# One operand of the first branch product: split ahead of its phase, or loaded once and split inside its first pair

## The chip, the cores and the metric

The kernel runs on one core of one Trainium2 chip. The metric is device time in microseconds (us) of that core, the median of several executions. Before the change it is 2460.27 us (3 runs, 2459.79 to 2461.08).

## The reference, cut to what matters

One decoder layer on 576 tokens (512 of a prompt, 64 of 8 samples), model width 2048, all in float32. The work is matrix products against weights:

```python
h = rmsnorm(x, norm_g)
proj = h @ w_in                              # ga, gb, cB, cC, cx, cg, q, k, v, gg, lr
za = cB * conv(cC * cx) * silu(cg)           # causal conv of width 3
branch_a = za @ w_branch_a                   # 2048 x 2048
zb = headRMSNorm(gla(q, k, v, lr)) * silu(gg)
branch_b = zb @ w_branch_b                   # 2048 x 2048
merged = sigmoid(ga) * branch_a + sigmoid(gb) * branch_b
y = rmsnorm(x + merged @ w_out, final_norm_g)
```

The change concerns `za @ w_branch_a` alone, and of that one operand made from `za`.

## The kernel before, in words

**Products in float32r, in three passes.** A float32 operand is kept as two tiles: hi, a rounded copy in float32r that ScalarE (ACT) writes, and lo, the difference between the value and hi, that VectorE (DVE) writes after it. A product is hi·hi + lo·hi + hi·lo: three groups of matmuls.

**Seven products for eight.** From 724 us on, every matrix product of two 128-column tiles against 2048 rows is done by a scheme of Strassen's kind: a *pair* of output tiles takes seven products (`PRODUCTS`, p = 0 to 6) of half size, each of 24 matmuls of 288 columns (8 slices of the contraction, 3 passes). There are 76 pairs: 52 on `w_in` (pairs 0 to 51), 8 on `w_branch_a` (from `PAIR_A` = 52), 8 on `w_branch_b` (from `PAIR_B` = 60), 8 on `w_out` (from `PAIR_C` = 68). The weights of each product are pieces `a11, a21, a12, a22` (tiles `pa`), loaded by DMAs that SyncE (SP) issues at L649, or sums of pieces that DVE makes at L1998 to L2007 (`add_pieces`). ACT rounds them into a ring of three tiles (`ring_hi`, L1107) and DVE subtracts (`ring_lo`, L1988). Three products share a ring, so this runs two products ahead of TensorE (PE).

**The activation operands.** Each of the seven products has its own activation operand, 128 x 8 x 288, stationary in SBUF during a phase, in one of seven slots: `act_y` quarters (`y11` to `y22`) or `act_x` quarters (0 to 3); `SLOTS` says which, for each phase. A slot holds hi and lo. While a phase's last pair runs, each slot comes free after its product, and SP loads the next phase's operand into it. Two ways exist for that:
- *plain*: one DMA (L672) brings the float32 values from `zt_d` into the lo half, then ACT rounds them into the hi half (L1437) and DVE subtracts in place (L2701). The steps at which ACT and DVE do this are the keys of `SPLITS`: the key counts products from the first one of the phase's previous pair, so -4 to 6 lie before the new phase's first pair (the *seam pair*, whose products have keys 7 to 13), and 8 and 10 in it.
- *ahead* (`AHEAD`): some pairs earlier, POOL's queue loads the values into a slot that is free for a while (`load_ahead`), ACT and DVE split them there, POOL's queue stores hi and lo to `zs_d` (`store_ahead`), and at the seam SP loads both halves ready made (L670), two DMAs of 1152 KB in place of one, with no work for ACT or DVE.

In the first pair of a phase PE takes the three passes one after the other (`late`), eight matmuls each: hi·hi needs the operand's hi, the second pass needs `ring_lo`, and the third the operand's lo (`x_lo`).

**What sets the order.** The five engines run instruction streams written out by hand, in order, with semaphores between them. In the loop over products g, DVE does in this sequence: the combination of results of the product before (L2498 to L2515 in the first branch), `add_pieces` for g + 3, `ring_lo` for g + 2, and then any operand split that `SPLITS` puts at this step. ACT does: saving of a result (L1309), `ring_hi` for g + 2, then the split. SP issues the piece `a21` of the next pair once `ring_lo` of product 4 of this pair is done, and `a12` after product 5.

Throughout, "product 6" is the seventh, and the seam is the one between the `w_in` pairs and the first pair of `w_branch_a`. Its PE work begins at 1883.05 us.

Of the kernel before, what the change touches and what calls it, by code (L numbers as in the profile page):

```python
# [55 lines left out]
         (3, "y12", "y11", 0, 1, "y21", 2),  # L56
         ("y22", 3, "y12", "y11", 0, 1, "y21"))

AHEAD = ((4, 6), (4, 6))

SPLITS = ({-35: 4, -21: 6, -4: 0, 4: 1, 6: 2, 8: 3, 10: 5},
          {-35: 4, -21: 6, -4: 0, 4: 1, 6: 2, 8: 3, 10: 5})


# [5 lines left out]
PAIR_A, PAIR_B, PAIR_C = PAIRS_G, PAIRS_G + PAIRS_B, PAIRS_G + 2 * PAIRS_B  # L70
# [8 lines left out]
SPLIT_WAY = (4, 2)  # L79
# [16 lines left out]
def hybrid_kernel(nc, x_prompt, x_sample, state_conv, state_gla, norm_g, w_in, conv_w, w_alpha2,  # L96
# [40 lines left out]
    zt_d = nc.dram_tensor("zt_d", [2, NPROD, P, KH, HALF], F32, kind="Internal").ap()  # L137
    zs_d = nc.dram_tensor("zs_d", [2, len(AHEAD[1]), 2, P, KH, HALF], F32, kind="Internal").ap()
    o_d = nc.dram_tensor("o_d", [KT, P, T], F32, kind="Internal").ap()
# [8 lines left out]
    with ctx:  # L148
# [306 lines left out]
        def slot_of(slot, b, f32=False):  # L455

            if isinstance(slot, int):
                return (x_f32 if f32 else act_x)[:, slot, 1 - b, :, :]
            kh, j = int(slot[1]) - 1, int(slot[2]) - 1
            return (y_f32 if f32 else act_y)[:, kh * KH:(kh + 1) * KH, b, j * HALF:(j + 1) * HALF]  # L460

        def aheads(f):


            return sum(len(AHEAD[n]) for n in range(f + 1))

        def split_count(f, p):


            return 4 + NPROD * f + list(SPLITS[f].values()).index(p) + 1  # L470

# [40 lines left out]
        def closed_before(u):  # L512

            return sum(closing[:u])

        def gates_before(u, par):

            return sum(FIRST[v][0] in ("ga", "gb") for v in range(par, u, 2))
# [64 lines left out]
        def landed(p):  # L583


            return 16 * (2 + 2 * (p in AHEAD[0]) + 1 + (p in SPLIT_WAY or p == 1))

        def place(m):

# [26 lines left out]
        def _(sp):  # L616
# [35 lines left out]
            def load_operand(f, p):  # L652

                slot = SLOTS[f + 1][p]
                if f == 2:
# [6 lines left out]
                    else:  # L662

                        for k0, k1 in ((0, KH - 2), (KH - 2, KH - 1)) if p == 1 else ((0, KH - 1),):
                            sp.wait_ge(way_out, 32 * k1)
                            sp.dma_start(slot_of(slot, 1, True)[:, k0:k1, :],
                                         zw_d[WAY[p] - KH // 2][:, k0:k1, :]).then_inc(blk_in[p], 16)
                elif p in AHEAD[f]:
                    for b in range(2):
                        sp.dma_start(slot_of(slot, b).bitcast(F32), zs_d[f, AHEAD[f].index(p), b]).then_inc(blk_in[p], 16)  # L670
                else:
# [51 lines left out]
        def _(pool):  # L723
# [97 lines left out]
            def load_o(m):  # L821


                pool.dma_start(mix[(m + 1) % 2][:, :, :], o_d.rearrange("(a m) p t -> m p a t", a=2)[m]
                               ).then_inc(o_in[m % 2], 16)
# [22 lines left out]
            def load_ahead(f, n):  # L848


                slot = SLOTS[f + 1][0]
                pool.wait_ge(ahead_out, 32 * (aheads(f - 1) + n))
                pool.dma_start(slot_of(slot, 1, True),
                               zt_d[f, STORED.index(PRODUCTS[AHEAD[f][n]].split()[1])]).then_inc(ahead_in, 16)

            def store_ahead(f, n):

                slot = SLOTS[f + 1][0]
                pool.wait_ge(x_lo, split_count(f, AHEAD[f][n]))
                for b in range(2):  # L860
                    pool.dma_start(zs_d[f, n, b], slot_of(slot, b).bitcast(F32)).then_inc(ahead_out, 16)
# [5 lines left out]
            for u in range(PAIR_A):  # L867

                if u and closing[u - 1]:
                    n = closed_before(u - 1)  # L870
                    store_z(n)
                    if n == 3:
                        store_tails(0)
                    if n == KH - 1:
                        store_tails(1)
                    if n >= KH - 1 and n + 2 < 2 * KH:
                        pool.wait_ge(z_out, 48 * (n + 1))
                        load_o(n + 2 - KH)
                if u == U_X - 1:
                    pool.wait_ge(conv_done, KH)  # L880
                    load_o(0)
                if u and FIRST[u - 1][0] in ("ga", "gb"):
                    store_gates(u - 1)
                if u == PAIR_A - 7:
                    pool.wait_ge(z_out, 48 * sum(closing))
                    pool.wait_ge(tail_out, 16 * 16)
                    load_ahead(0, 0)
                if u == PAIR_A - 5:
                    store_ahead(0, 0)
                    load_ahead(0, 1)  # L890
                if u == PAIR_A - 3:
                    store_ahead(0, 1)
            pool.wait_ge(gate_out[0], 16 * gates_before(PAIR_A, 0))
            load_gate(0, 2 * A_PAIRS[0])
            load_gate(0, 2 * A_PAIRS[0] + 1)
# [155 lines left out]
        def _(act):  # L1051
# [333 lines left out]
            for u in range(NPAIR):  # L1385
                kind = kind_of(u)
                last = kind_of(u - 1) if u else "branch"
                for p in range(NPROD):
# [40 lines left out]
                    for h, start in ((1, PAIR_A), (2, PAIR_B)):  # L1429
                        q = SPLITS[h - 1].get(g - (start - 1) * NPROD)  # L1430
                        if q is not None:
# [446 lines left out]
        def _(dve):  # L1878
# [783 lines left out]
            for u in range(NPAIR):  # L2662
                kind = kind_of(u)
                last = kind_of(u - 1) if u else "branch"
                for p in range(NPROD):
# [30 lines left out]
                    for h, start in ((1, PAIR_A), (2, PAIR_B)):  # L2696
                        q = SPLITS[h - 1].get(g - (start - 1) * NPROD)
                        if q is not None:
# [116 lines left out]
```

## Time and profile before

| | |
|---|---|
| median of 3 runs | 2460.27 us |
| the profiled execution, its own time | 2461.4 us |
| its span | 2459.6 us |
| PE busy | 2419.8 us, 98% |
| DVE busy | 1852.7 us, 75% |
| ACT busy | 1072.9 us, 44% |
| DMA moved | 369.04 MB, mean 150 GB/s |

PE is the engine that is nearly always at work; busy shares of the others say little by themselves. Matmuls overlap, so 24 of them of some 0.295 us each take about 3.2 us. What matters is where PE waits, and for whom. In a timeline a row gives the start, the length, the engine, the line and tiles, the count, and in brackets how long the engine sat idle before it and who released it.

### The profile page before, as it was taken

What the parts mean: (1) busy time and instruction counts of PE and PEld (TensorE: products, weight loads), DVE (VectorE), ACT (ScalarE), POOL (GpSimd) and SP (SyncE); (2) the same over time, 40 slices, a digit from 0 to 9 for tenths busy, and PEclk for the clock granted to TensorE, in tenths of its full rate; (3) what the DMA queues carried; (4) which work ended last, traced back from release to release, by engine and by line L of the source; (5) the groups of instructions that cost most, each with busy time, mean ns of one, the idle gap of its engine ahead of it and who ended that gap; (6) DMA issues with size and microseconds to landing.
All of it is one profiled execution on the core that took longest, in us unless ns stands there. A gap on an engine that the chain in (4) does not pass through costs nothing.

```text
span 2459.6 us, 43962 instructions
## 1 busy us (share of the span) xinstructions
PE 2419.8 (98%) x18106; PEld 2369.7 (96%) x18106; DVE 1852.7 (75%) x2723; ACT 1072.9 (44%) x1614; POOL 277.4 (11%) x474
## 2 busy tenths in 40 slices
PE   8999999999999999999999999999999999999996
PEld 7998989999899999999999999999999999999996
DVE  7556667575688787877878888876667778999776
ACT  6343444434443443444444344444445445445443
POOL 3002121020210000000000011100000110332111
PEclk9999999999999999999999999999999999999998
DMA  7225345252533443443333445654578679669555
GB/s 204 79 60 175 111 134 153 77 184 81 186 102 103 120 115 87 108 122 103 101 106 103 130 120 160 182 147 120 161 216 272 216 221 295 191 194 296 142 162 161
DMA packets 456249, 369.04 MB, mean 150 GB/s; under 512 B 15989, under 2 KB 425761, under 8 KB 453537
## 3 DMA queue, kind: packets, MB, share of 16 engines
q1 hardware_dynamic: 419826, 238.91, 35.2%
q0 software_dynamic: 36224, 127.32, 15.7%
q8 instruction: 144, 2.36, 0.4%
q14 instruction: 55, 0.45, 0.1%
HBM read 286.50 MB, written 79.68 MB: 149 GB/s over the span
## 4 chain that ended last, share of the span: by engine, by line
PE 92%; DVE 3%; DMA 2%; issue 1%; ACT 1%; SPq 0%; POOL 0%; DVEq 0%; ACTq 0%; POOLq 0%
PE bank L1867 37%; PE acc L1867 28%; PE acc L1717 20%; PE acc L1673 1%; PE acc L1602 1%; DVE ring_lo L1988 1%; PE bank L1670 1%; PE bank L1646 1%; DMA x_rows<-in_x_prompt 1%; PE bank L1634 1%; PE bank L1667 1%; DMA x_f<-zw_d 0%; DMA pa<-in_w_branch_a 0%; PE bank L1589 0%; PE acc L1770 0%
## 5 line engine op out<-in xcount | busy, mean ns | idle before, releaser
L1988 DVE TENSOR_TENSOR ring_lo<-pa,ring_hi 128x1024 fp32r<-128x1024 f32 x532 | 649.6, 1221 | 201.5 <-ACT ring_hi L1107 198.2
L1107 ACT ACTIVATE ring_hi<-pa 128x1024 fp32r<-128x1024 f32 x532 | 561.7, 1056 | 373.1 <-PE bank L1867 214.9
L1717 PE MATMUL acc<-act_y,w_hi 128*128 128x288 f32 x2560 | 519.8, 298 | 0.0
L1867 PE MATMUL bank<-act_y,ring_hi 128*128 128x288 f32 x2432 | 478.3, 295 | 1.9 <-DMA act_y<-zs_d 1.1
L1867 PE MATMUL bank<-act_x,ring_hi 128*128 128x288 f32 x2432 | 475.8, 294 | 2.3 <-ACT act_x L1365 1.2
L1867 PE MATMUL acc<-act_x,ring_hi 128*128 128x288 f32 x2176 | 435.4, 294 | 1.3 <-DVE ring_lo L1988 1.3
L1717 PEld LDWEIGHTS acc<-act_y,w_hi 128*128 128x128 f32 x2560 | 410.9, 189 | 2.6 <-issue 1.2
L1867 PEld LDWEIGHTS bank<-act_x,ring_hi 128*128 128x128 f32 x2432 | 387.5, 189 | 3.5 <-ACT act_x L1365 1.7
L1867 PEld LDWEIGHTS bank<-act_y,ring_hi 128*128 128x128 f32 x2432 | 385.1, 189 | 3.1 <-DMA act_y<-zs_d 1.4
L1717 PE MATMUL acc<-act_y,w_lo 128*128 128x288 f32 x1280 | 377.9, 295 | 0.0
L1867 PEld LDWEIGHTS acc<-act_x,ring_hi 128*128 128x128 f32 x2176 | 351.1, 189 | 1.8 <-issue 1.5
L1867 PE MATMUL bank<-act_x,ring_lo 128*128 128x288 f32 x1216 | 344.5, 296 | 0.6 <-DVE ring_lo L1988 0.5
L1867 PE MATMUL bank<-act_y,ring_lo 128*128 128x288 f32 x1216 | 342.9, 295 | 0.0
L1867 PE MATMUL acc<-act_x,ring_lo 128*128 128x288 f32 x1088 | 322.3, 296 | 0.0
L1867 PE MATMUL acc<-act_y,ring_hi 128*128 128x288 f32 x1472 | 295.6, 295 | 3.8 <-DVE ring_lo L1988 3.8
L1717 PEld LDWEIGHTS acc<-act_y,w_lo 128*128 128x128 f32 x1280 | 242.0, 189 | 0.0
L1867 PEld LDWEIGHTS acc<-act_y,ring_hi 128*128 128x128 f32 x1472 | 236.0, 189 | 4.7 <-issue 4.4
L1867 PEld LDWEIGHTS bank<-act_x,ring_lo 128*128 128x128 f32 x1216 | 222.7, 188 | 1.0 <-DVE ring_lo L1988 1.0
L1867 PEld LDWEIGHTS bank<-act_y,ring_lo 128*128 128x128 f32 x1216 | 223.2, 188 | 0.0
L1867 PE MATMUL acc<-act_y,ring_lo 128*128 128x288 f32 x736 | 217.1, 295 | 0.0
L1867 PEld LDWEIGHTS acc<-act_x,ring_lo 128*128 128x128 f32 x1088 | 204.1, 188 | 0.0
L1309 ACT ACTIVATE part<-acc 128x288 f32<-128x288 f32 x152 | 62.5, 411 | 264.5 <-PE acc L1867 264.4
(369 smaller groups left out, 2701.9 us busy)
## 6 DMA issues: line engine op xcount, KB each, us to landing
pa<-in_w_in SPq DMA_DIRECT2D x208, 512.0 KB, 5.3
raw<-in_w_in SPq DMA_DIRECT2D x40, 1024.0 KB, 5.7
pa<-in_w_branch_a SPq DMA_DIRECT2D x32, 512.0 KB, 6.1
pa<-in_w_branch_b SPq DMA_DIRECT2D x32, 512.0 KB, 6.9
pa<-in_w_out SPq DMA_DIRECT2D x32, 512.0 KB, 6.8
states<-in_state_gla POOLq DMA_DIRECT2D x48, 256.0 KB, 3.4
out<-states POOLq DMA_DIRECT2D x48, 256.0 KB, 2.5
zt_d<-gate_tile POOLq DMA_DIRECT2D x12, 576.0 KB, 3.5
```

Source lines behind the costliest of these rows:

```text
L1107: A(ring_hi[g % RING][:, :], piece_of[src][u % 2][:, :], ACT.Copy).then_inc(part_hi, 1)
L1309: A(dst[:, :], psum_of(u)[b], ACT.Copy).then_inc(part_saved, 1)
L1602: mm = nc.tensor.matmul(b_gram[:, a * P:(a + 1) * P], dec[:, kk, a * P:(a + 1) * P], dec[:, kk, MID + a * P:MID + (a + 1) * P], start=(kk ...
L1634: nc.tensor.matmul(b_smp[r:r + TS // 2, :], q_pad[:, a % 2, kk, b, :], state_of(2 * a + b)[:, kk, :], start=(a == 0), stop=(a == NS // 2 - 1))
L1646: mm = nc.tensor.matmul(bank[:, kk, :], kd_one[:, kk * P:(kk + 1) * P], v2[:, j // (NS // 2), :], start=True, stop=True)
L1667: nc.tensor.matmul(out, v_rows[:, b, v * P:(v + 1) * P], scores[:, b * P:(b + 1) * P], start=True, stop=(c == 0))
L1670: nc.tensor.matmul(out, s_prompt[:, kk, v * P:(v + 1) * P], qe[:, kk, b * P:(b + 1) * P], start=False, stop=(kk == KK - 1))
L1673: mm = nc.tensor.matmul(b_chunk[kk], kd_rows[:, b, kk * P:(kk + 1) * P], v_rows[:, b, :], start=True, stop=True)
L1717: mm = nc.tensor.matmul(half_bank[h % 2][:, 0:HALF], (w_hi, w_lo)[a][par][:, k * P:(k + 1) * P], y_of(k, b, j), start=(k == 0 and n == 0), ...
L1867: mm = nc.tensor.matmul(out, (ring_hi, ring_lo)[a][r][:, k * P:(k + 1) * P], slot_of(slot, b)[:, k, :], start=(p in (0, 1, 3) and k == 0 a ...
L1988: V.tensor_tensor(ring_lo[g % RING][:, :], piece_of[source_of(g)][u % 2][:, :], ring_hi[g % RING][:, :].bitcast(F32), ALU.subtract).then_i ...
```

## The change

Product 6's operand of the first branch leaves `AHEAD` and becomes a plain one. Its split by ACT and DVE moves from key -21 (product 0 of the pair three before the last `w_in` pair) to key 12 (product 5 of the seam pair). Its slot is `y22`. POOL's queue loses one load and two stores; SP's queue has one load (L672) where it had two (L670). Products of the second branch are as they were; counts of semaphores (`landed`, `split_count`) follow.

```diff
-AHEAD = ((4, 6), (4, 6))
+AHEAD = ((4,), (4, 6))
-SPLITS = ({-35: 4, -21: 6, -4: 0, 4: 1, 6: 2, 8: 3, 10: 5},
+SPLITS = ({-35: 4, -4: 0, 4: 1, 6: 2, 8: 3, 10: 5, 12: 6},
           {-35: 4, -21: 6, -4: 0, 4: 1, 6: 2, 8: 3, 10: 5})
...
         def landed(p):
-            return 16 * (2 + 2 * (p in AHEAD[0]) + 1 + (p in SPLIT_WAY or p == 1))
+            return 16 * (sum(1 + (p in names) for names in AHEAD) + 1 + (p in SPLIT_WAY or p == 1))
...
                 if u == PAIR_A - 5:
                     store_ahead(0, 0)
-                    load_ahead(0, 1)
-                if u == PAIR_A - 3:
-                    store_ahead(0, 1)
```

DVE's instructions in the seam pair, products 4 to 6, before. `ring_lo` rows are the lo parts of weights, `pa` rows the sums of pieces, `mix_tile` rows the combination of results:

```order
L2498 TENSOR_TENSOR mix_tile<-bank,part_82 128x288
L2500 TENSOR_TENSOR mix_tile<-mix_tile,gate_tile 128x288
L1988 TENSOR_TENSOR ring_lo_65<-pa_0_57,ring_hi_62 128x1024
L2504 TENSOR_TENSOR mix_tile<-part_81,part_79 128x288
L2506 SCALAR_TENSOR_TENSOR mix_tile<-mix_tile,gate_tile 128x288
L1998 TENSOR_TENSOR pa_59<-pa_59,pa_1_58 128x1024
L1988 TENSOR_TENSOR ring_lo_66<-pa_1_56,ring_hi_63 128x1024
L2510 TENSOR_TENSOR mix_tile<-bank,part_80 128x288
L2511 TENSOR_TENSOR mix_tile<-mix_tile,gate_tile 128x288
L2003 TENSOR_TENSOR pa_1_56<-pa_1_56,pa_59 128x1024
```

And now (line numbers are three lower, since the file has three lines less):

```order
L2495 TENSOR_TENSOR mix_tile<-bank,part_82 128x288
L2497 TENSOR_TENSOR mix_tile<-mix_tile,gate_tile 128x288
L1985 TENSOR_TENSOR ring_lo_65<-pa_0_57,ring_hi_62 128x1024
L2501 TENSOR_TENSOR mix_tile<-part_81,part_79 128x288
L2503 SCALAR_TENSOR_TENSOR mix_tile<-mix_tile,gate_tile 128x288
L1995 TENSOR_TENSOR pa_59<-pa_59,pa_1_58 128x1024
L1985 TENSOR_TENSOR ring_lo_66<-pa_1_56,ring_hi_63 128x1024
L2698 TENSOR_TENSOR act_y<-y_f_86,act_y 128x8x288
L2507 TENSOR_TENSOR mix_tile<-bank,part_80 128x288
L2508 TENSOR_TENSOR mix_tile<-mix_tile,gate_tile 128x288
L2000 TENSOR_TENSOR pa_1_56<-pa_1_56,pa_59 128x1024
```

The operand's subtraction (L2698, in before L2701) now stands behind the sum of pieces L1995, which needs the piece `a21` of the next pair (tile `pa_59`), and behind one `ring_lo`.

SP's queue around the seam, before, from the last pieces ahead of the seam:

```order
L649 DMA pa_1_58<-in_w_branch_a 128x8x128
L670 DMA act_y<-zs_d 128x8x288 x2
L672 DMA x_f_88<-zt_d 128x2304
L670 DMA act_y<-zs_d 128x8x288 x2
L649 DMA pa_59<-in_w_branch_a 128x8x128
```

and now:

```order
L649 DMA pa_1_58<-in_w_branch_a 128x8x128
L670 DMA act_y<-zs_d 128x8x288 x2
L672 DMA x_f_88<-zt_d 128x2304
L672 DMA y_f_86<-zt_d 128x8x288
L649 DMA pa_59<-in_w_branch_a 128x8x128
```

The order is the same; product 6's load, between product 5's (`x_f`) and the piece `a21` (`pa_59`), is one DMA and not two.

## Rows read from the trace of the kernel before

**Rows 1.** The page: busy time, share of the span, instructions.
```profile
PE 2419.8 (98%) x18106; PEld 2369.7 (96%) x18106; DVE 1852.7 (75%) x2723; ACT 1072.9 (44%) x1614; POOL 277.4 (11%) x474
```

**Rows 2.** Waits of PE, 1895 to 1930: total, times, longest.
```profile
PE bank L1867 <- DMA act_y<-zs_d: 1.1, 1, 1.1
PE acc L1867 <- DVE ring_lo L1988: 0.9, 1, 0.9
```

**Rows 3.** Timeline of PE in the seam pair and the start of the next.
```profile
1883.05 1.22 PE L1867 MATMUL bank<-act_y,ring_hi 128*128 128x288 f32 x8
...
1901.32 1.33 PE L1867 MATMUL bank<-act_x,ring_hi 128*128 128x288 f32 x8
1903.79 1.32 PE L1867 MATMUL bank<-act_y,ring_hi 128*128 128x288 f32 x8 [1.14 <-DMA act_y<-zs_d]
1904.95 1.22 PE L1867 MATMUL bank<-act_y,ring_lo 128*128 128x288 f32 x8
1906.01 1.22 PE L1867 MATMUL bank<-act_y,ring_hi 128*128 128x288 f32 x8
1908.09 0.51 PE L1867 MATMUL acc<-act_y,ring_hi 128*128 128x288 f32 x2 [0.87 <-DVE ring_lo L1988]
```

**Rows 4.** The chain that ended last: start, us, what.
```profile
1895.39 10.17 DMA pa<-in_w_branch_a
```

**Rows 5.** Windows at the old split: length, busy PE, PEld, DVE, ACT, POOL, PEclk, DMA.
```profile
1790.00:1800.00 10.00, 10.00 (x77) 10.00 (x77) 6.98 (x6) 6.35 (x8) 0.71 (x1) 1.00 0.77 236
```

**Rows 6.** Timeline of SP's queue: issues of the seam's loads.
```profile
1884.44 1.57 SPq L672 DMA_DIRECT2D x_f<-zt_d  x1
1886.06 7.46 SPq L670 DMA_DIRECT2D act_y<-zs_d  x2
```

**Rows 7.** The same DMAs by window: count, KB each, median us to landing.
```profile
x_f<-zt_d SPq DMA_DIRECT2D x1, 1152.0 KB, 12.1
act_y<-zs_d SPq DMA_DIRECT2D x1, 1152.0 KB, 14.0
act_y<-zs_d SPq DMA_DIRECT2D x1, 1152.0 KB, 17.1
```

**Rows 8.** Timeline of DVE in the seam pair.
```profile
1898.71 2.56 DVE L2701 TENSOR_TENSOR act_x<-x_f,act_x 128x2304 fp32r<-128x2304 f32 x1 [2.13 <-ACT act_x L1437]
...
1903.67 0.46 DVE L2506 SCALAR_TENSOR_TENSOR mix_tile<-mix_tile,gate_tile 128x288 f32<-128x288 f32 x1
1905.58 1.22 DVE L1998 TENSOR_TENSOR pa<-pa,pa 128x1024 f32<-128x1024 f32 x1 [1.46 <-DMA pa<-in_w_branch_a]
1906.72 1.22 DVE L1988 TENSOR_TENSOR ring_lo<-pa,ring_hi 128x1024 fp32r<-128x1024 f32 x1
1907.86 0.45 DVE L2510 TENSOR_TENSOR mix_tile<-bank,part 128x288 f32<-128x288 f32 x1
```

**Rows 9.** Timeline of ACT in the seam pair.
```profile
1896.55 2.13 ACT L1437 ACTIVATE act_x<-x_f 128x2304 fp32r<-128x2304 f32 x1 [1.23 <-DMA x_f<-zt_d]
...
1899.82 1.05 ACT L1107 ACTIVATE ring_hi<-pa 128x1024 fp32r<-128x1024 f32 x1
1906.84 1.06 ACT L1107 ACTIVATE ring_hi<-pa 128x1024 fp32r<-128x1024 f32 x1 [5.97 <-DVE pa L1998]
```

**Rows 10.** Windows at the start and the tail (columns as in rows 5).
```profile
37.50:37.70 0.20, 0.20 (x2) 0.20 (x2) 0.20 (x2) 0.20 (x2) 0.03 (x1) 0.68 0.00 0
38.00:41.00 3.00, 3.00 (x16) 3.00 (x16) 2.97 (x6) 0.00 (x0) 2.50 (x5) 0.50 0.39 106
41.00:41.20 0.20, 0.20 (x4) 0.20 (x3) 0.20 (x2) 0.00 (x0) 0.00 (x0) 1.00 0.18 56
...
2443.50:2444.50 1.00, 0.00 (x0) 0.00 (x0) 0.93 (x5) 0.20 (x1) 0.00 (x0) 0.73 0.82 229
```

**Rows 11.** Timeline of PE before the first fall of its clock, and at the tail.
```profile
36.20 1.34 PE L1529 MATMUL acc<-ident,x_rows 64*128 64x64 f32 x16
...
2441.10 0.52 PE L1770 MATMUL bank<-ident,mix_tile 128*128 128x128 f32 x3 [0.59 <-ACT mix_tile L1383]
```

## The prediction

> **What bounds the kernel now.** I read the page first: PE is busy 98% of the span, so an edit pays only where PE waits [rows 1]. Then the waits of PE by window. Between 1750 and 1895 us there is none, so the place of the old split costs nothing today; between 1895 and 1930 there are two, one in the seam pair and one at the pair after it [rows 2]. Then the timelines of the engines in that stretch. The reader is to see in PE's that product 5's third pass starts at 1901.32, product 6 at 1903.79 after a wait for its two zs_d loads, and the next pair at 1908.09 after a wait for `ring_lo` [rows 3]. Passes follow each other at 1.06 us when nothing is late (1904.95 to 1906.01) and at 1.16 us after a wait (1903.79 to 1904.95) [rows 3]. From 1883.05 to 1901.32 there are 17 passes, 1.07 us each; 21 of them take 22.5 us, so unhindered the next pair would start at 1905.5: this seam loses 2.6 us in all. The chain that ended last explains the second wait: the piece a21 was issued at 1895.39, took 10.17 us [rows 4], and then DVE's sum of pieces and `ring_lo` followed [rows 8].
>
> **What the change removes.** (a) Early: one load, one ACT split, one DVE split and two stores, near 1786 to 1830 us. In the 10 us that hold the old split PE is busy for 10.00 at full clock, DVE for 6.98 and ACT for 6.35 [rows 5]. Worth 0. POOL's queue loses three issues there, and nothing waits for that queue in that stretch but POOL itself. (b) At the seam: one of two 1152 KB loads. They were issued from 1886.06, the second about 1886.6 [rows 6], and landed after 14.0 and 17.1 us, at 1900.1 and 1903.7; product 5's load, issued at 1884.44, landed after 12.1 us, at 1896.5; the piece a21, issued at 1895.39, after 10.17 us, at 1905.6 [rows 4, 6, 7]. So they land in the order of issue, 3.6 us apart for 1152 KB and 1.9 us for 512 KB. With one load gone product 6's values land at about 1900.1 and a21 at about 1900.1 + 1.9 = 1902.0. Product 5's load is ahead of the removed one and lands as before, at 1896.5, so ACT's and DVE's split of product 5 stay where they are (1896.55 and 1898.71) [rows 8, 9].
>
> **What it adds, step by step.** ACT: its `ring_hi` of 1899.82 ends at 1900.87, the values are there since 1900.1, and the split takes 2.13 us, as product 5's did [rows 9]. Hi is ready at 1903.0. ACT was idle for 5.97 us at that place, until 1906.84 [rows 9], so the split delays nothing on ACT. Product 5 ends at 1901.32 + 1.16 = 1902.5; PE starts product 6 at 1903.05, 0.7 us earlier than now, and its second pass ends at 1903.05 + 1.16 + 1.06 = 1905.3.
> DVE is the term that decides. It is in order, and the subtraction is queued behind L1998 and one L1988. L2506 starts at 1903.67 and takes 0.46 us [rows 8]; instructions in a row start some 0.08 us before the former's listed end (L1998 at 1905.58, L1988 at 1906.72, next at 1907.86: 1.14 us apart for 1.22 listed). L1998 waited 1.46 us for a21 [rows 8]; with a21 there at 1902.0 it starts at 1904.05. L1988 (the next pair's product 0) starts at 1905.19, the new subtraction at 1906.33. It takes 2.56 us, as product 5's [rows 8], and ends at 1908.9. PE's third pass of product 5 started 0.05 us after such an end (1898.71 + 2.56 = 1901.27 against 1901.32 [rows 3, 8]), so product 6's third pass starts at 1908.95, and the next pair, 1.16 us later, at 1910.1. Its `ring_lo` was ready at 1906.4, so that wait of 0.87 us is gone.
> Sum: 1910.1 - 1908.09 = +2.0 us. By waits: the start of product 6 was 1903.79 - 1902.5 = 1.3 us late and that of the next pair 1908.09 - (1906.01 + 1.06) = 1.0; both go. In their place come 0.55 for hi (1902.5 to 1903.05) and 3.65 for lo (1905.3 to 1908.95), and 0.1 for one more restart.
> Behind the subtraction on DVE stand the combination for product 5 (L2510, L2511), the sum L2003 and `ring_lo` for the next pair's product 1. They start 1.0 us later than now (1908.8 for 1907.86): 0.9 + 1.14 + 1.14 after that, `ring_lo` is ready at about 1912.1, and PE wants it at 1910.1 + 3.2 = 1913.3. Hidden with 1.2 us to spare. Were it not, PE would wait for the difference. POOL's store of mix_tile moves by 1 us and is wanted a pair later. From 1910.1 on all runs as before, 2.0 us later: the later seams wait for DVE and DMAs that themselves follow PE's counts, so I let nothing be given back.
>
> **Bounds.** If a21 lands no earlier than now (1905.58), the sum is +2.0 + 1.5 = +3.5. If product 5's load came earlier by the 1.23 us that ACT waited [rows 9], DVE's whole row moves up by that: +0.8. If the subtraction were hidden altogether and both old waits gone, the seam's whole loss: -2.6. I take +2.0, as the four landings [rows 4, 7] stand in order of issue with even steps.
>
> **PE's clock.** The granted clock is at 2.4 GHz (1.00) through the seam, with waits of 1.1 us and less. It fell to 1.2 GHz (0.50) twice: at about 37.6 us, after 1.3 us of 64-column transposes, and within 2443.5 to 2444.5 (mean 0.73, so near 2443.96), 2.3 us after the end of PE's last matmul, 2441.10 + 0.52 [rows 10, 11]. The first time it stayed low for 3.4 us (37.6 to 41.0) [rows 10]. The new wait of 3.65 us is longer than the 2.3 us without matmuls after which the tail lost the clock. So a fall is well possible here, and would cost half of the matmul time spent at the low level: 3.4 / 2 = 1.7 us, as a bound from the one stretch seen.
> The Trainium skill, "TensorE: Matmul & The Clock Gate", section "HAM oscillation — how this bites in real kernels", says that a matmul loop that stops for its operand comes back at the half clock each time. By that rule the sum would be +3.7; by the waits of this seam, which kept 1.00, it would be +2.0. The tail agrees with the rule, the seam's shorter waits do not reach it.
>
> **The rivals.**
> 1. *The clock falls in the new wait.* For it: the tail. Against it: part of the low stretch would lie inside the wait, where it costs nothing, and this wait has matmuls close on both sides. +2.0 + 1.7 = +3.7: 2464.0. This is also the one way over the bound to slower: it decides when the low clock covers 2 x (4.9 - 2.0) = 5.8 us of matmuls, 1.7 times the stretch seen [rows 10], or 2.8 us of them with a21 late. Then 2465.2 and more.
> 2. *The seam's DMAs aren't relieved in time*: a21 still lands at 1905.6, the engines being held by the load that stays as they were by two. For it: 10.17 us for 512 KB show how much stands in the queue [rows 4], and no row shows it with one load less. Against it: the order and the steps of the landings [rows 4, 7]. +3.5: 2463.8.
> 3. *DVE gets to the subtraction earlier*, product 5's load being helped too: +0.8, 2461.1. Against it: that load was issued ahead of the removed one.
> 4. *The relief wins*: product 6's lo in time, both waits gone: -2.6, 2457.7. Against it: DVE has 1.14 + 1.14 + 2.56 us to do from 1904.05, and nothing on DVE can be skipped. For a gain DVE would need to end by 1906.9.
> 5. *It doesn't do what it says*: the splits stand in the order shown, so this is left to nothing.
>
> **How the numbers follow.** The profiled execution took 2461.4 us for a span of 2459.6, 1.1 us above the median. On its own time the forecast is 2463.4, on the median 2460.27 + 2.0 = 2462.3. Chances: forecast 0.50, rival 1 0.25 (0.05 of it over the bound), rival 2 0.10, rival 3 0.10, rival 4 0.03, anything unnamed 0.02. What a measurement can tell from no change is 0.2%, 4.9 us: 2455.4 to 2465.2. All cases but the tail of rival 1 and half of the unnamed lie inside it: faster 0.02, same 0.92, slower 0.06. The range leaves out rival 4 and rival 1's tail and has 0.6 us for the runs' own spread (2459.79 to 2461.08): 2460.3 to 2465.2.
>
> **What would show it.** Right: PE waits before product 6's third pass for DVE's act_y at L2698, some 3.6 us; the waits for zs_d and for `ring_lo` are gone; DVE's L1995 has no idle time ahead of it; the next pair starts about 27.0 us after the seam's first matmul (25.04 now). Wrong: L1995 waits for `pa` (rival 2), PEclk under 1.00 in the windows behind the wait (rival 1), or PE's wait under 2 us with the next pair starting at under 25 us (rival 4). A difference outside -1 to +5 us, or one that arises anywhere else than in these 27 us, would make the prediction wrong.

## The result, and the profile after

| | before | changed |
|---|---|---|
| median, 20 runs each | 2460.7 us (2459.11 to 2463.2) | 2464.64 us (2462.63 to 2467.99) |
| ratio | | 1.0016, 95% interval 1.0010 to 1.0022 |
| profiled execution, span | 2459.6 us | 2461.2 us |
| DMA moved | 369.04 MB | 364.32 MB |

The changed kernel is 3.9 us slower, 2.5 to 5.4 by the interval; a second set of runs (11 of the changed kernel, 33 of before) gave the same ratio, 1.0016 (1.0007 to 1.0024), with medians 4.9 us apart. That is 0.16%, inside the 0.2% that the forecast called no change; the forecast was +2.0 us, 2462.3. The kernel's time thus fell where a rival of the forecast had put it (+3.7, 2464.0), not where its likeliest case had.

The two profiled spans differ by 1.6 us only. The difference has to be read between two places of the program, not from zero, because one profile of a kernel differs from another ahead of the seam: in the profile of before the clock was low from 37.6 to 41.0 us [rows 10], in that of the changed kernel it was not, and its seam starts 1.94 us earlier, at 1881.11. Profiles that had the same at the start agree: with no fall of the clock there the seam begins at 1881.11 in the changed kernel and 1881.36 in a second profile of before, with one at 1882.87 and 1883.05 against 1883.05. Places below are therefore counted from the seam's first matmul.

PE's waits from 1870 to 1960 us in the changed kernel (total, times, longest), to be held against [rows 2]:

```profile
PE bank L1864 <- DVE act_y L2698: 3.6, 1, 3.6
PE bank L1864 <- ACT act_y L1434: 0.3, 1, 0.3
```

Both old waits are gone, and two new ones stand in their place. PE's timeline answers to [rows 3]:

```profile
1881.11 1.22 PE L1864 MATMUL bank<-act_y,ring_hi 128*128 128x288 f32 x8
...
1899.27 1.33 PE L1864 MATMUL bank<-act_x,ring_hi 128*128 128x288 f32 x8
1900.88 1.32 PE L1864 MATMUL bank<-act_y,ring_hi 128*128 128x288 f32 x8 [0.28 <-ACT act_y L1434]
1902.04 1.21 PE L1864 MATMUL bank<-act_y,ring_lo 128*128 128x288 f32 x8
1906.87 2.17 PE L1864 MATMUL bank<-act_y,ring_hi 128*128 128x288 f32 x8 [3.62 <-DVE act_y L2698]
1908.83 0.69 PE L1864 MATMUL acc<-act_y,ring_hi 128*128 128x288 f32 x2
```

Product 6 starts 19.77 us after the seam's first matmul (before: 20.74), its third pass at 25.76 (22.96), the next pair at 27.72 (25.04). Note the lengths: eight matmuls listed at 2.17 us instead of 1.22, and two at 0.69 instead of 0.51. Those ran at half the clock, 1.2 GHz. The starts of two neighbours at either level:

```profile
1909.31 0.45 PE L1864 MATMUL acc<-act_y,ring_lo 128*128 128x288 f32 x1
1909.55 0.69 PE L1864 MATMUL acc<-act_y,ring_hi 128*128 128x288 f32 x2
...
1910.63 0.29 PE L1864 MATMUL acc<-act_y,ring_lo 128*128 128x288 f32 x1
1910.76 0.43 PE L1864 MATMUL acc<-act_y,ring_hi 128*128 128x288 f32 x2
```

They are 0.24 us apart at 1.2 GHz and 0.13 at 2.4 (0.240 and 0.132 over the whole row of starts): a low stretch does not double a matmul's time here but makes it 1.8 times as long. DVE's timeline, to [rows 8], and ACT's, to [rows 9]:

```profile
1896.65 2.56 DVE L2698 TENSOR_TENSOR act_x<-x_f,act_x 128x2304 fp32r<-128x2304 f32 x1 [2.02 <-ACT act_x L1434]
...
1901.61 0.46 DVE L2503 SCALAR_TENSOR_TENSOR mix_tile<-mix_tile,gate_tile 128x288 f32<-128x288 f32 x1
1901.99 1.22 DVE L1995 TENSOR_TENSOR pa<-pa,pa 128x1024 f32<-128x1024 f32 x1
1903.12 1.22 DVE L1985 TENSOR_TENSOR ring_lo<-pa,ring_hi 128x1024 fp32r<-128x1024 f32 x1
1904.26 2.55 DVE L2698 TENSOR_TENSOR act_y<-y_f,act_y 128x2304 fp32r<-128x2304 f32 x1
```

```profile
1897.76 1.05 ACT L1104 ACTIVATE ring_hi<-pa 128x1024 fp32r<-128x1024 f32 x1
1898.71 2.12 ACT L1434 ACTIVATE act_y<-y_f 128x2304 fp32r<-128x2304 f32 x1
1903.24 1.06 ACT L1104 ACTIVATE ring_hi<-pa 128x1024 fp32r<-128x1024 f32 x1 [2.42 <-DVE pa L1995]
```

DVE runs without a gap from 1896.65 on: L1995 no longer waits for a21, and the subtraction is the fourth instruction behind L2501. ACT was done with hi at 1900.83, 3.4 us before DVE came to it. SP's queue and landings (count, KB, us), to [rows 6, 7]:

```profile
1883.95 0.53 SPq L672 DMA_DIRECT2D y_f<-zt_d  x1
1893.44 31.82 SPq L649 DMA_DIRECT2D pa<-in_w_branch_a  x8
```

```profile
y_f<-zt_d SPq DMA_DIRECT2D x1, 1152.0 KB, 14.1
pa<-in_w_branch_a SPq DMA_DIRECT2D x1, 512.0 KB, 6.5
```

The values landed at 1898.05, a21 at 1899.9, after 6.5 us in place of 10.17 [rows 4]. And the clock, by windows (columns as in [rows 5]):

```profile
1903.20:1906.80 3.60, 0.05 (x1) 0.00 (x0) 3.60 (x4) 1.06 (x1) 0.00 (x0) 1.00 0.37 110
1907.10:1910.40 3.30, 3.30 (x15) 3.30 (x15) 3.27 (x6) 1.06 (x1) 1.10 (x2) 0.50 0.23 89
1910.50:1914.00 3.50, 3.50 (x28) 3.50 (x28) 2.09 (x2) 1.01 (x2) 1.60 (x3) 1.00 0.87 245
```

After 3.6 us in which PE did nothing the granted clock was 1.2 GHz for 3.4 us: 15 matmuls in 3.30 us, against 28 in 3.50 us behind it.

### The profile page after: what moved, and what is told of

It is laid out like the page before. It is cut to its first block, busy times and chain, and to the rows that moved or that the text cites. A ratio compares the mean times of both kernels' runs of the same rounds, so it can differ in the third digit from the quotient of the medians.

```text
span 2461.2 us, 43958 instructions
## 1 busy us (share of the span) xinstructions
PE 2419.8 (98%) x18106; PEld 2369.2 (96%) x18106; DVE 1853.3 (75%) x2723; ACT 1072.5 (44%) x1614; POOL 274.6 (11%) x471
## 2 busy tenths in 40 slices
DMA packets 454393, 364.32 MB, mean 148 GB/s; under 512 B 15925, under 2 KB 424673, under 8 KB 451681
## 4 chain that ended last, share of the span: by engine, by line
PE 93%; DVE 3%; DMA 2%; issue 1%; ACT 1%; SPq 0%; POOL 0%; DVEq 0%; ACTq 0%
PE bank L1864 37%; PE acc L1864 28%; PE acc L1714 20%; PE acc L1670 1%; PE acc L1599 1%; PE bank L1667 1%; DVE ring_lo L1985 1%; PE bank L1643 1%; PE bank L1631 1%; PE bank L1664 1%; DMA x_f<-zt_d 1%; DMA x_rows<-in_x_prompt 0%; DMA x_f<-zw_d 0%; PE bank L1586 0%; PE acc L1767 0%
```

## The experiments

Two theories were put to the test. Theory 1: the +3.9 us are the late lo of product 6 (+2.0) and the clock that falls over the wait for it (up to +1.7). Theory 2: the fall in one profile is chance, and much of the difference comes from elsewhere. Each edited kernel was profiled once, and b_relief, a_late_lo, a_load_twice and a_lo_before_sum were also timed only once, so that only their profiles are read. The table gives the starts in us after the seam's first matmul, from PE's timelines. "Next pair" is the one that follows the seam pair, "pair after" the one behind that: by then all that the seam costs has been paid. Profiles of one kernel differ by 0.1 us (before) to 0.4 us (changed) in these columns, so differences of that size say nothing.

| kernel | product 6 | its third pass | next pair | pair after | clock low within the seam or next pair |
|---|---|---|---|---|---|
| before, 1st / 2nd profile | 20.74 / 20.65 | 22.95 / 22.87 | 25.03 / 24.94 | 47.35 / 47.25 | no / no |
| changed, 1st / 2nd / 3rd | 19.77 / 19.70 / 19.99 | 25.76 / 25.69 / 25.97 | 27.72 / 27.70 / 28.05 | 50.71 / 50.63 / 50.69 | yes / yes / yes |
| a_fill24 | 19.59 | 25.53 | 26.70 | 48.93 | no |
| a_key11 | 19.55 | 22.57 | 25.79 | 49.64 | yes |
| a_key11_lo_first | 19.48 | 22.57 | 23.80 | 48.07 | no |
| b_relief | 19.31 | 21.42 | 23.37 | 45.67 | no |
| a_late_lo | 19.59 | 21.80 | 23.12 | 45.44 | no |
| a_load_twice | 22.76 | 27.27 | 28.44 | 50.72 | yes |
| a_lo_before_sum | 19.58 | 23.22 | 25.58 | 49.17 | yes |
| b_lo_first | 20.53 | 22.74 | 23.79 | 46.02 | no |
| b_lo_first_one | 20.74 | 22.95 | 24.01 | 46.24 | no |

Each low stretch ahead of the tail lasted 3.41 us.

**The kernels themselves, again.** The changed kernel, timed 11 times and profiled twice more, and the kernel before with a second profile. No edit.

> The changed kernel again, unchanged, as the measure for the others. Theory 1 (the late lo of product 6 costs 2.0 us, and PE's wait for it lets the clock fall to 1.2 GHz, which costs up to 1.7 us more): the next pair starts 27.0 us (clock held) to 27.8 us (clock fallen) after the seam's first matmul, the pair after that 49.3 to 51.0 us (before: 25.03 and 47.35); total +2 to +4 us over before. Theory 2 (the clock's fall in the profile is chance and the +3.9 us of the timed runs come from elsewhere, from the stages ahead of the seam or behind it): total about +3.9 us, with no more than +2.0 us of it between the seam's first matmul and the second pair behind it when the clock is held.

> The changed kernel, for a third profile. Theory 1: the clock falls again in or right behind the wait of 3.6 us, as in the two profiles so far (next pair at +27.7 us, the pair after at +50.6 us). Theory 2: no fall this time, the pair after at +48.9 us.

> The kernel before, for a second profile of it. Theory 1: through the seam of product 6 the clock stays at 1.00, since PE waits 1.1 us at most there; next pair at +25.0 us, the pair after at +47.35 us. It may show falls of the clock at the start or at the last seam, 1.7 us each, which would be the spread between runs of one kernel. Theory 2: the clock falls at this seam in the kernel before as well.

Measured: 2466.35 us (11 runs) against 2461.43 (33 runs), ratio 1.0016 (1.0007 to 1.0024). In all three profiles of the changed kernel the clock fell 25.5 to 25.9 us after the seam's first matmul, within 0.5 us of PE's restart; in neither of the two of before did it fall there. The pair after comes 3.3 to 3.4 us later than in before, and from there on both kernels keep their distance: the first matmul of the `w_out` phase is at 363.59 and 363.57 us in before, at 367.05, 367.16 and 367.02 in the changed kernel, +3.4 to +3.6. So the seam holds the difference. Falls occur elsewhere too, in both kernels: near the start (before's first profile, the changed kernel's second and third) and at the last seam (before's second, the changed kernel's second). Each run's mean granted clock is listed as well, and it counts the falls: in the 14 profiles it was 0.997 only in the two in which the clock fell nowhere ahead of the tail. It was 0.997 in 14 of the 33 runs of before and in none of the 31 runs of the changed kernel (20 and 11), so in each of those 31 the clock fell at least once ahead of the tail, though the runs don't say where. Among runs with 0.996 the medians are 2462.49 (15 runs) and 2464.61 us (6), a difference of 2.1.

What the fall costs can be read in the changed kernel's own profiles. With the clock held, the pair after follows the third pass of product 6 by 23.40 us (a_fill24 below: 25.53 to 48.93). In the changed kernel it followed by 24.95, 24.94 and 24.72 us. So the clock cost 1.5, 1.5 and 1.3 us, and what is left of the distance to before, 1.8 to 2.1 us, is the late lo. A low stretch full of matmuls takes 3.41 / 0.240 = 14 of them, 0.108 us more each: 1.5 us.

**Matmuls to fill the wait (a_fill24).**

```diff
                         if late and k == 0 and n == 2 and fresh:
+                            if u == PAIR_A and p == 6:
+                                for j in range(24):
+                                    nc.tensor.matmul(acc[1][:, 0:HALF], ring_hi[r][:, j % KH * P:(j % KH + 1) * P],
+                                                     slot_of(slot, 0)[:, j % KH, :], start=True, stop=True)
                             pe.wait_ge(x_lo, fresh)
```

> 24 matmuls of 288 columns into an unused PSUM tile, between the second and the third pass of product 6 in the seam pair: 24 x 0.133 = 3.2 us of the 3.6 us in which PE waits for lo. Theory 1: DVE ends at the same time, so lo is as late as before, but the clock stays at 1.00; next pair at +27.0 us, the pair after at +49.3 us, total +2.0 us over before, 1.5 to 2 us below the changed kernel. Theory 2: the filler saves nothing, total +3.9 us as the changed kernel, and the next pair starts no earlier.

Measured: 2463.42 us, 2.9 below the median of the changed kernel timed beside it; ratio to before 1.0006 (0.9998 to 1.0015). The pair after came at 48.93 where I had expected 49.3. PE's timeline, the third row being the filler:

```profile
1903.59 1.32 PE L1868 MATMUL bank<-act_y,ring_hi 128*128 128x288 f32 x8 [0.27 <-ACT act_y L1434]
1904.74 1.22 PE L1868 MATMUL bank<-act_y,ring_lo 128*128 128x288 f32 x8
1905.79 3.32 PE L1865 MATMUL acc<-act_y,ring_hi 128*128 128x288 f32 x24
1909.53 1.33 PE L1868 MATMUL bank<-act_y,ring_hi 128*128 128x288 f32 x8 [0.42 <-DVE act_y L2702]
```

```profile
1907.00:1910.00 3.00, 2.58 (x20) 2.35 (x19) 2.96 (x4) 0.00 (x0) 0.00 (x0) 1.00 0.06 17
1910.00:1914.00 4.00, 4.00 (x33) 4.00 (x32) 4.00 (x5) 1.06 (x1) 1.82 (x4) 1.00 0.37 128
```

The lo is as late as before the edit, PE does 3.2 us of work that nobody reads, and the kernel gets faster: the clock stays at 2.4 GHz (1.00). The pair after is at 48.93, 1.8 us earlier than in the changed kernel and 1.6 later than in before. Of the 1.8 us some 0.2 were there already when the third pass began (25.53 for 25.76), ahead of any effect of the clock, which leaves 1.5 to 1.6 for the clock. The timed runs agree: the mean clock was 0.997 in 5 of 11 runs, and their median, 2461.97 us, is 1.7 above that of the runs of before with 0.997 (2460.29, 14 runs), which is the late lo with no fall anywhere. Theory 2 is out.

**Relief alone (b_relief).** The kernel before, the seam's second DMA for product 6 cut to one slice of eight (the kernel leaves out the loads of the other seven of its lo):

```diff
                     for b in range(2):
-                        sp.dma_start(slot_of(slot, b).bitcast(F32), zs_d[f, AHEAD[f].index(p), b]).then_inc(blk_in[p], 16)
+                        k1 = 1 if (f, p, b) == (0, 6, 1) else KH
+                        sp.dma_start(slot_of(slot, b).bitcast(F32)[:, 0:k1, :],
+                                     zs_d[f, AHEAD[f].index(p), b][:, 0:k1, :]).then_inc(blk_in[p], 16)
```

> The kernel before with the second of product 6's two zs_d loads at the seam cut to one eighth (its lo half, slices 1 to 7 not loaded and so left out of the result). The relief of the DMAs alone, with no work for ACT or DVE. By the forecast's landings: hi and the rest are there at 17.1 us after the seam's first matmul, a21 about 2 to 3 us earlier than before; product 6 starts at 19.4 us with no wait (before 20.74), ring_lo of the next pair 1.4 us earlier; next pair at +22.7 to +23.0 us (before 25.03), the pair after at +45.1 (before 47.35). Rival (the DMA relief is worth nothing, DVE and not a21 was what made ring_lo late): product 6 starts on time, but the next pair no earlier than +24 us.

Measured: product 6 without a wait at 19.31, the next pair at 23.37, the pair after at 45.67: -1.7 us. The next pair came 0.4 us later than expected:

```profile
1906.85 0.50 PE L1869 MATMUL acc<-act_y,ring_hi 128*128 128x288 f32 x2 [0.72 <-DVE ring_lo L1990]
```

`ring_lo` is still 0.72 us late with a21 in time, by its place behind product 5's split, two combinations and a sum on DVE. The relief is worth 1.7 of the 2.6 us that I had as the seam's whole loss.

**All of it but DVE's subtraction (a_late_lo).** The changed kernel, with DVE's subtraction moved to key 16, and hi taken for lo in the third pass (the kernel leaves out the product of hi and the operand's lo there):

```diff
-                        q = SPLITS[h - 1].get(g - (start - 1) * NPROD)
+                        key = g - (start - 1) * NPROD
+                        q = SPLITS[h - 1].get(key)
+                        if h == 1 and key in (12, 16):
+                            q = 6 if key == 16 else None
...
-                        if late and k == 0 and n == 2 and fresh:
+                        away = u == PAIR_A and p == 6 and n == 2
+                        if late and k == 0 and n == 2 and fresh and not away:
                             pe.wait_ge(x_lo, fresh)
+                        if u == PAIR_A + 1 and p == 6 and (n, k) == order[0]:
+                            pe.wait_ge(x_lo, split_count(0, 6))
...
-                                              slot_of(slot, b)[:, k, :],
+                                              slot_of(slot, 0 if away else b)[:, k, :],
```

> The changed kernel with DVE's subtraction for product 6 done four products later, in the next pair, and hi taken in place of lo in the third pass of the seam's product 6 (the hi x lo part of that one product is left out). All of the change but DVE's subtraction in the seam. Forecast: only ACT's hi is late, 0.3 to 0.5 us; next pair at +22.9 us, clock held; the pair after at +45.3 us, or up to 1.5 us more if the moved subtraction meets DVE's work there. Rival (the wait in the third pass is for something else, ACT or DMA): next pair at +26 us or more.

Measured: 23.12 and 45.44, with one wait at this seam, for ACT's hi:

```profile
1902.97 1.32 PE L1867 MATMUL bank<-act_y,ring_hi 128*128 128x288 f32 x8 [0.27 <-ACT act_y L1434]
```

So all of the change but this one instruction is a gain of 1.9 us, and the instruction in its place costs 48.93 - 45.44 = 3.5 us with the clock held, 1 us more than the 2.55 us that it takes. Four products later DVE has room for the same 2.55 us at no cost.

**The bytes put back (a_load_twice).** The changed kernel with product 6's values loaded twice:

```diff
+                    src = zt_d[f, STORED.index(PRODUCTS[p].split()[1])]
+                    if (f, p) == (0, 6):
+                        sp.dma_start(slot_of(slot, 0).bitcast(F32), src).then_inc(blk_in[p], 16)
-                    sp.dma_start(slot_of(slot, 1, True),
-                                 zt_d[f, STORED.index(PRODUCTS[p].split()[1])]).then_inc(blk_in[p], 16)
+                    sp.dma_start(slot_of(slot, 1, True), src).then_inc(blk_in[p], 16)
...
```

The counts of semaphores for product 6 follow (not shown).

> The changed kernel with product 6's values loaded twice at the seam (first into the hi half, where ACT then writes), so that the queue carries as many bytes as before the change. By the forecast's bound: the values land at 20.6 us after the seam's first matmul, hi is ready at 22.8 us (3.1 us later than in the changed kernel), a21 lands at 22.5 us and DVE's sum waits 1.4 us for it; DVE's subtraction ends 1.4 us later than in the changed kernel, at 27.2 us; next pair at +28.3 (clock held) to +29.5 us. Rival (the transfers don't decide anything here): as the changed kernel, +27.7 us.

Measured: next pair at 28.44. ACT's and DVE's rows:

```profile
1903.77 2.12 ACT L1436 ACTIVATE act_y<-y_f 128x2304 fp32r<-128x2304 f32 x1 [2.88 <-DMA y_f<-zt_d]
```

```profile
1905.58 1.23 DVE L1997 TENSOR_TENSOR pa<-pa,pa 128x1024 f32<-128x1024 f32 x1 [1.44 <-DMA pa<-in_w_branch_a]
1906.72 1.22 DVE L1987 TENSOR_TENSOR ring_lo<-pa,ring_hi 128x1024 fp32r<-128x1024 f32 x1
1907.86 2.55 DVE L2700 TENSOR_TENSOR act_y<-y_f,act_y 128x2304 fp32r<-128x2304 f32 x1
```

The values landed 20.6 us after the seam's first matmul, at 1903.7, and a21 kept DVE for 1.44 us: the landings that the forecast had worked out by order of issue, and the bound of +3.5 us for a21 unrelieved (28.44 - 25.03 = 3.4). The clock fell here too, at 1905.63, during the first wait. It cost nothing: PE's first two passes ran at half rate inside the time in which DVE's lo was awaited anyway, as the timeline shows with 2.29 and 1.68 us and a further wait behind them:

```profile
1905.95 2.29 PE L1866 MATMUL bank<-act_y,ring_hi 128*128 128x288 f32 x8 [3.28 <-ACT act_y L1436]
1908.03 1.68 PE L1866 MATMUL bank<-act_y,ring_lo 128*128 128x288 f32 x8
1910.46 1.33 PE L1866 MATMUL bank<-act_y,ring_hi 128*128 128x288 f32 x8 [0.75 <-DVE act_y L2700]
```

**DVE's order: the subtraction first (a_lo_before_sum).** At key 12, the subtraction ahead of `add_pieces(g + 3)` and `split_lo(g + 2)`:

```diff
                         stage(v, q)
+                    if u == PAIR_A and p == 5:
+                        slot = SLOTS[1][6]
+                        dve.wait_ge(x_hi, split_count(0, 6))
+                        V.tensor_tensor(slot_of(slot, 1), slot_of(slot, 1, True), slot_of(slot, 0).bitcast(F32),
+                                        ALU.subtract).then_inc(x_lo, 1)
                     if g and g + 3 < NG and product_at(g + 3) in (1, 2, 4, 5):
                         add_pieces(g + 3)
...
-                        if q is not None:
+                        if q is not None and (h, q) != (1, 6):
```

> The changed kernel with DVE's subtraction for product 6 ahead of the sum of pieces and of ring_lo, at the same step. If the order on DVE is what makes lo late: the subtraction starts 2.3 us earlier, third pass at 23.4 us after the seam's first matmul (25.7 in the changed kernel), but ring_lo of the next pair then ends at 25.7 us: next pair at +25.8 us, and the pair after at +48.0 us (no more than 0.7 us over before), clock held or fallen by chance (+1.7). Rival (it is ACT's hi or the landing that makes it late): third pass at 25.7 us as before.

Measured: third pass at 23.22 for the 23.4 expected, next pair at 25.58, pair after at 49.17, of which 1.5 at most is the clock's, which fell at 1906.13. The order on DVE made lo late, not ACT or the landing. Here the clock fell with waits of only 1.24 and 1.04 us behind each other:

```profile
1904.38 1.32 PE L1864 MATMUL bank<-act_y,ring_hi 128*128 128x288 f32 x8 [1.24 <-DVE act_y L2671]
1906.74 0.82 PE L1864 MATMUL acc<-act_y,ring_hi 128*128 128x288 f32 x2 [1.04 <-DVE ring_lo L1985]
```

**One product earlier (a_key11), and with `ring_lo` first (a_key11_lo_first).**

```diff
-SPLITS = ({-35: 4, -4: 0, 4: 1, 6: 2, 8: 3, 10: 5, 12: 6},
+SPLITS = ({-35: 4, -4: 0, 4: 1, 6: 2, 8: 3, 10: 5, 11: 6},
```

and, for the second alone, on DVE:

```diff
+                    early = u == PAIR_A and p == 5
+                    if early:
+                        split_lo(g + 2)
                     if g and q >= 3:
...
-                    if g + 2 < NG:
+                    if g + 2 < NG and not early:
                         split_lo(g + 2)
```

> The split of product 6's operand one product earlier (key 11 for 12), on ACT and DVE. Theory 1: ACT starts it when the values land, about 17.0 us after the seam's first matmul, DVE at 20.0 us, straight behind ring_lo of product 6, ends at 22.6 us; the third pass waits 0.7 us; then ring_lo of the next pair's first product is what comes late, behind the sum of pieces, at 25.7 us. Next pair at +25.7 us (0.7 us over before), clock held, total +0.7 us. Theory 2: total +3.9 us, since the seam's waits are not its cause.

> As the run with key 11, and on DVE ring_lo of the next pair's first product goes ahead of the combination and the sum of pieces at that step. Theory 1: that ring_lo ends at 23.8 us after the seam's first matmul, when PE's third pass of product 6 ends; next pair at +23.9 us, 1.1 us less than before and 3.8 less than the changed kernel; total -1.1 us against before. Theory 2: total +3.9 us.

Measured: 2463.94 us, 1.0008 (0.9999 to 1.0017), and 2462.38 us, 1.0001 (0.9993 to 1.0010). Up to the next pair both came as expected, 25.79 and 23.80. Behind it they did not. In the first the clock fell, at 1910.16, behind waits of 0.7 and 1.9 us. It does not fall in every run: the mean clock was 0.997 in 2 of 11 runs of a_key11 and in 6 of 11 of a_key11_lo_first. In the second DVE's backlog came out one product later:

```profile
PE acc L1864 <- DVE ring_lo L1985: 1.7, 1, 1.7
PE bank L1864 <- DVE act_y L2701: 0.7, 1, 0.7
```

The pair after was at 48.07, 0.7 us later than in before, where I had expected 46.2 (-1.1). Against a_late_lo (45.44) these are 2.6 us, the length of the subtraction: with DVE busy throughout, 2.5 us more of work come out late. The other two orders come to much the same once the fall is taken off at 1.5 us (an estimate): 48.1 for a_key11, 47.7 or a little more for a_lo_before_sum. Only the order of the change costs 3.5 to 3.9. So the order decides over 1 us of the lateness, over where the wait stands, and, by the falls, over the clock; the rest comes out late in any order tried.

**`ring_lo` first in the kernel before (b_lo_first, b_lo_first_one).** The same DVE edit as above, without the change, with `u in (PAIR_A, PAIR_B)` in the one and `u == PAIR_A` in the other.

> The kernel before, with one change on DVE at the first two seams: at product 5 of the seam pair, ring_lo of the next pair's first product goes ahead of the combination and of the sum of pieces that waits for a21. If ring_lo was late only by its place behind that sum: the wait of 0.87 us goes, next pair at +24.1 us (25.03), the pair after at +46.4 us (47.35), at the second seam another 0.3 to 1.2 us; total -1 to -2 us against before. Rival: DVE is full there, so that what is won is given back at the next ring_lo, and the pair after starts at +47.3 us; total 0.

> The kernel before with ring_lo ahead of the combination and the sum at product 5 of the first seam pair only, not at the second seam, where the profile of b_lo_first showed a new wait of 3.12 us and a fall of the clock. If what was won at the first seam there (next pair at +23.8 us, the pair after at +46.0 us, 1.3 us before the kernel before) was given back at the second: here the pair after the seam at +46.0 us, first matmul of the third branch's phases at its old distance, total -1.3 us against before. Rival: the 1.3 us are lost again somewhere behind the first seam: total 0, with the profile showing where.

Measured: b_lo_first 2462.11 us, 1.0005 (0.9996 to 1.0014). At the first seam it wins 1.3 us (46.02). At the second the pair behind the seam starts 1.5 us sooner, but then the rival holds: the combination, six short instructions there, pushes the following `ring_lo` back, PE waits

```profile
2091.62 0.51 PE L1867 MATMUL acc<-act_y,ring_hi 128*128 128x288 f32 x2 [3.12 <-DVE ring_lo L1988]
```

and the clock falls at 2092.01; the phase of `w_out` starts at 363.85, 0.3 later than in before. With the first seam alone (b_lo_first_one) the gain stays: 46.24 for 47.35, and 362.61 for 363.59 at the start of `w_out`. PE's only wait there from 1870 to 1960 us is

```profile
PE bank L1867 <- DMA act_y<-zs_d: 1.1, 1, 1.1
```

Its median is 2459.94 us against 2461.89, ratio 0.9994 (0.9985 to 1.0003). By the profile it is 1.0 us faster than before, and that is less than the runs can tell from none.

## Why the prediction was right, and where it was not

The class, no change, and the range came true. The likeliest case did not: what happened is rival 1, and the range holds it because it had been drawn to take that rival in.

- *The old split's place is worth nothing.* The distance between the kernels arises in the seam alone, as said; the stages ahead differ from profile to profile by the clock near the start, in both kernels, and from 1881.11 to 1881.36 where it kept 1.00.
- *The relief.* Landings were forecast at 17.05 us after the seam's first matmul for the values and 18.95 for a21; measured 16.94 and 18.8. Both old waits are gone. Alone it is worth 1.7 us (b_relief), 1.9 with the new hi (a_late_lo); the two differ by no more than profiles of one kernel do. Rival 2 is out by a21's landing, rival 3 by DVE's split of product 5, which began 15.54 us after the seam's first matmul, for 15.66 before, and rival 4 by the wait of 3.62 us.
- *ACT's hi.* Forecast 0.55 us late, counted from 1.16 us after the start of product 5's third pass. Counted so, it was 0.45 (1900.88 against 1899.27 + 1.16); the 0.28 of the row is counted from the listed end of the pass. The forecast let the split begin at the listed end of `ring_hi`; it began 0.1 us ahead of it (1898.71 against 1897.76 + 1.05), and ACT and DVE were another 0.1 us ahead of before's times.
- *DVE's lo.* Forecast: third pass at 25.90, a wait of 3.65, next pair at 27.05. Measured: 25.76, 25.69 and 25.97 in three profiles, and a wait of 3.8 counted as the forecast counts it (1906.87 against 1902.04 + 1.06; the row lists 3.62). With 1.16 us to the next pair, as with the clock held, that is 26.9, 26.9 and 27.1; a_fill24 has 26.70. As a sum, +2.0 was forecast; measured are +1.8 to +2.1 in the changed kernel's profiles and +1.6 in a_fill24. The mechanism, its place and its size were right.
- *Nothing is late behind it.* Right in the changed kernel, and in a_fill24, where the clock held: no wait between the third pass and the pair after. The spare of 1.2 us was real but small, as a_key11_lo_first showed once the next pair came earlier.
- *The clock.* This is where the likeliest case failed. I gave 0.50 to a clock that holds and 0.25 to the fall, which occurred in three of three profiles; by the mean clock, each of the 31 timed runs had at least one fall. The step that failed is the weighing of the seam's shorter waits, at which the clock kept 1.00, and of the low stretch lying in part inside the wait. It fell 0.2 and 0.1 us after PE's restart in two profiles and 0.5 ahead of it in the third, so nearly all of the 3.41 us was paid. The price, 1.7 us, was half of the stretch; measured are 1.3 to 1.5, since a matmul takes 0.240 us at the low level and 0.132 at the full one, not twice as long. And the tail, on which rival 1 rested, was one profile's: in the 14 profiles here the clock fell 2.3 to 4.1 us after the end of PE's last matmul. The 2.3 us lay at the low end, and that was luck: the second profile of before has 3.7 us, longer than the forecast wait, and would have spoken against the fall. The rule of the Trainium skill, "TensorE: Matmul & The Clock Gate", section "HAM oscillation — how this bites in real kernels", by which a matmul loop that stops for its operand comes back at half clock, was borne out by the wait of 3.6 us, in three of three profiles. The Trainium skill tells it there of long waits; at those of before, 1.1 and 0.9 us, the clock kept 1.00. The forecast's sum by that rule, +3.7, is nearer to the measured +3.9 than my +2.0.
- *The sum.* 1.8 to 2.1 for the lo and 1.3 to 1.5 for the clock are 3.4 us in the profiles (3.3 to 3.6 at the later places). The runs say 3.9 with an interval from 2.5 to 5.4. The half microsecond between them is inside the interval; whether more falls at other seams add to it is open. A forecast of +2.0 that had priced the fall by these rows would have been +3.5.
- *The chances of the classes.* Outside the bounds lie 0.05 of rival 1 and half of the unnamed 0.02, which is 0.06 in all; faster 0.02 and slower 0.06 together say 0.08.

## What to carry to other kernels

Where PE is the bound, a wait can cost more than its length (here 3.6 us and then 1.3 to 1.5): ask of every new wait whether the clock comes back low behind it, and compare an edit by the distance between two places of the program, since a fall at the start or at a seam moves the whole profile: the seam here begins at 1881.10 to 1882.02 us in the five profiles without a fall near the start and at 1882.70 to 1884.00 in the nine with one. Work that an engine has room for on average can still be late: what counts is what stands ahead of it in that engine's order between its input and the moment it is wanted. In a stretch where that engine has no gap, reordering took 1 us off the lateness at best and moved the rest (pair after +0.4 to +0.8 with the fall taken off, for +1.6 to +2.1); taking the work out of the stretch removed all of it (-1.9).

## What was not expected

- Filler matmuls that nobody reads took 2.9 us off the median of the changed kernel (2466.35 to 2463.42, 11 runs each), by keeping the granted clock at 1.00.
- The clock fell in one kernel with two waits of 1.24 and 1.04 us (a_lo_before_sum), in another with 0.7 and 1.9 (a_key11), and held in another with 0.74 and 1.69 (a_key11_lo_first); before's 1.1 and 0.9 kept it in both of its profiles. Each edited kernel has one profile here, and the clock differs from run to run. What tells these apart was not settled.
- In the one such profile, a fall inside a wait cost nothing as the work at half clock ended before the next thing that PE waited for (a_load_twice).
